# Unread rounded products of 512 columns ahead of the attention scores of a three-layer transformer kernel

## The reference

```python
# first layer
o_gla  = gla_chunked(q, k, v, g)          # 4 heads, dk 64, dv 128, chunks of 64
o_moba = moba_attention(q_b, k_b, v_b)    # 4 heads of 64, causal softmax with ALiBi
o_mem  = memory_attention(q_c, k_c, v)    # 4 heads of 64, 256 memory tokens
x = x + concat(o_gla, o_moba, o_mem) @ w_out
x = x + hierarchical_moe(rmsnorm(x, g), ...)   # 32 experts, 2 of them for each token
# second layer
ya = _diff_attention(...)                 # 4 heads, each with two softmaxes of 64 columns
yb = _dsa_attention(...)                  # 8 heads, 64 keys kept for each query by an index score
x = x + g1 * (concat(ya, yb) @ w_out);  x = x + g2 * swiglu(h)
# third layer
y = _swa_sink_attention(...)              # 16 heads, window of 128
x = x + g1 * (y @ w_out);               x = x + g2 * swiglu(h)
```

## Time and profile before

| what | value |
|---|---|
| time of the kernel, median of 3 runs | 1481.8 us (1477.46 to 1483.74) |
| time of the profiled execution | 1480.7 us |
| span of the profiled execution (first to last instruction) | 1478.7 us |
| PE busy | 1207.3 us, 82% of the span, 7691 MATMUL records |
| DVE busy | 615.7 us, 42% |
| ACT busy | 476.1 us, 32% |
| mean granted PE clock | 0.864 of full speed |
| DMA | 368.67 MB, mean 249 GB/s |

### The profile page before, as it was taken

How to read it: one execution, slowest core, us unless ns; L and a number is a source line. 1 busy time by engine, 2 the same in 40 slices (tenths; PEclk the granted TensorE clock), 3 DMA queues, 4 the chain that set the end, 5 groups by cost and what they waited for, 6 DMA issues and landing times.

```text
span 1478.7 us, 19441 instructions
## 1 busy us (share of the span) xinstructions
PE 1207.3 (82%) x7691; PEld 883.7 (60%) x7691; DVE 615.7 (42%) x1239; ACT 476.1 (32%) x769; POOL 7.6 (1%) x54
## 2 busy tenths in 40 slices
PE   5878886775676756847897888999999978999998
PEld 4655464442333323413675337899898734999986
DVE  3472643110010000101753576655535756565553
ACT  4561530100000000002532335554433447465441
POOL 1000000000000000000000000000000000000000
PEclk9897788888888877977897668899999988999999
DMA  8442347999999999999536431865536462665520
GB/s 292 172 152 76 115 173 320 428 430 429 430 430 428 430 430 428 430 425 403 197 129 228 171 114 58 253 207 201 195 145 226 171 253 90 203 196 174 203 109 29
DMA packets 121728, 368.67 MB, mean 249 GB/s; under 512 B 9842, under 2 KB 56093, under 8 KB 110878
## 3 DMA queue, kind: packets, MB, share of 16 engines
q1 hardware_dynamic: 120556, 367.26, 64.7%
q10 hardware_dynamic: 1074, 0.08, 0.1%
HBM read 366.28 MB, written 1.05 MB: 248 GB/s over the span
## 4 chain that ended last, share of the span: by engine, by line
PE 61%; DMA 21%; DVE 9%; ACT 5%; issue 3%; SPq 1%; DVEq 0%; ACTq 0%
PE ps L1810 58%; DMA more<-in_w_down_dram 7%; DMA more<-in_w_gate_dram 7%; DMA more<-in_w_up_dram 6%; PE ps L1814 3%; DVE st L32 2%; DVE ring_r L32 2%; DVE R_c L32 1%; SPq L664 1%; DVE R_a L32 1%; DVE X_c L32 1%; ACT X_c L32 1%; DVE sc L32 1%; ACT R_a L32 1%; ACT hn L32 1%
## 5 line engine op out<-in xcount | busy, mean ns | idle before, releaser
L1810 PE MATMUL ps<-hT_r,ring_r 128*128 128x256 f32 x864 | 245.5, 284 | 0.0
L1810 PE MATMUL ps<-ring,xg 128*32 128x512 f32 x640 | 140.4, 725 | 121.5 <-DMA more<-in_w_gate_dram 42.6
L1810 PEld LDWEIGHTS ps<-hT_r,ring_r 128*128 128x128 f32 x864 | 167.8, 194 | 0.0
L1810 PEld LDWEIGHTS ps<-ring,xg 128*32 128x32 f32 x640 | 35.2, 131 | 217.2 <-issue 217.2
L32 DVE TENSOR_TENSOR ring_r<-ring,W_c_r 128x1024 fp32r<-128x1024 f32 x94 | 115.2, 1226 | 97.5 <-ACT W_c_r L32 94.1
L1810 PE MATMUL ps<-R_c_r,W_c_r 128*128 128x256 f32 x608 | 153.1, 284 | 0.0
L32 DVE TENSOR_TENSOR ring_r<-ring,X_c_r 128x1024 fp32r<-128x1024 f32 x88 | 107.8, 1225 | 98.4 <-ACT X_c_r L32 95.7
L1810 PE MATMUL ps<-R_c_r,X_c_r 128*128 128x256 f32 x576 | 148.2, 285 | 0.0
L32 ACT ACTIVATE W_c_r<-ring 128x1024 fp32r<-128x1024 f32 x94 | 99.7, 1060 | 89.2 <-PE ps L1810 84.5
L32 ACT ACTIVATE X_c_r<-ring 128x1024 fp32r<-128x1024 f32 x88 | 93.3, 1061 | 90.3 <-PE ps L1810 85.4
L1810 PE MATMUL ps<-hT_r,W_c_r 128*128 128x256 f32 x416 | 119.0, 286 | 1.9 <-DVE R_c_r L32 1.8
(11 more groups left out here) (281 smaller groups left out, 1874.5 us busy)
## 6 DMA issues: line engine op xcount, KB each, us to landing
ring<-in_ada_w_dram SPq DMA_DIRECT2D x24, 2048.0 KB, 8.2
ring<-in_w_gate_dram SPq DMA_DIRECT2D x20, 2048.0 KB, 15.9
ring<-in_w_up_dram SPq DMA_DIRECT2D x20, 2048.0 KB, 20.7
ring<-in_w_down_dram SPq DMA_DIRECT2D x20, 2048.0 KB, 16.4
more<-in_w_up_dram SPq DMA_DIRECT2D x12, 2048.0 KB, 24.4
more<-in_w_gate_dram SPq DMA_DIRECT2D x12, 2048.0 KB, 23.1
more<-in_w_down_dram SPq DMA_DIRECT2D x12, 2048.0 KB, 23.6
ring<-in_ffn_gate_dram SPq DMA_DIRECT2D x22, 1024.0 KB, 5.6
```

Source lines behind the costliest of these rows:

```text
L1810: return pe.matmul(out, lhsT, rhs, start=start, stop=stop, skip_group_check=True)
```

## The change

A helper `keep(b)` is added to PE's program. It multiplies a rounded 128x128 piece of the activations `hT` by a rounded 128x512 piece of them, in one MATMUL, and writes all 512 columns of bank b. It is called ahead of each of the two score products of a unit in the attentions 1, 2 and 3 (48 calls), ahead of each score product of the gated attention (8) and ahead of the values of the gated attention (8): 64 products more. Each bank is overwritten by the product that follows (`start=True`), so that nothing reads what `keep` wrote. The call stands behind `take(b)`; in `gla_values` it stands ahead of the wait for the masked scores. Attention 4 is left as it was.

```diff
+            steady = hH[:, 0:2, :].rearrange("p c n -> p (c n)")
+
+            def keep(b):
+                mm(ps[b][:, :], hH[:, 0, 0:128], steady, True, True)
+
...
                         b = 2 * (U % 2) + m
                         take(b)
+                        if n < 4:
+                            keep(b)
                         mm(ps[b][:, 0:unit.nk], unit.q[m], unit.k[m], True, True).then_inc(s_sc, 1)
...
                 take(u % 4)
                 pe.wait_ge(s_gT, 1)
+                keep(u % 4)
                 mm(ps[u % 4][:, 0:128], gkT[r, hp, 128 * a:128 * a + 128], gqT[r, hp, 128 * a:128 * a + 128], True,
                    True).then_inc(s_gs, 1)
...
                 take(b)
+                keep(b)
                 pe.wait_ge(s_ga, u + 1)
                 pe.wait_ge(s_sst, 6)
```

## The result

The changed kernel takes **1504.5 us** (median of 4 runs, 1503.7 to 1507.0) against 1482.0 (1477.5 to 1483.7): ratio 1.0166, 95% interval 1.0147 to 1.0185, some 24 us slower (the two medians lie 22.5 us apart). I had forecast 1491 with a range that ended at 1504. The direction was right, the size was not. The profiled execution took 1503.7 us with a span of 1501.9, so the two traces are 23.2 us apart.

What follows compares the result with a forecast made beforehand. PE was taken to hold 61% of the chain and DMA 21%, with the experts bound by DMA. Terms -3.2 + 3.6 + 7.5 + 2.7 = +10.6 us on the profiled 1480.7 gave 1491, range 1479 to 1504.

Steps and rivals of the forecast that it cites:

- The price of one product: Each added 512-column product costs 0.23 us at 2.4 GHz and 0.43 at 1.2, read from a stream of rounded products.
- The price of splitting a pair: Parting a unit's two score products costs between 0 and 0.75 us at 256 columns, full clock; 0.45 taken.
- some 3 us: How much higher the whole sum would be if splitting lost the entire second score product, 0.75 instead of 0.45 a unit.
- Gated attention, -3.2: Twelve products on the path cost 2.8 us, attention 1's unit 0 costs 0.8; the held full clock saves 6.8.
- Rival B: Clock falls in the gated attention all the same, so its products do not pay: +21.8 us, 1502; chance 0.28.
- Attention 1, +3.6: Units 1 to 7: 0.9 for unit 1, 0.4 for 2 and 3, 3.6 for 4 to 7, less 1.3 won.
- The run that I had expected to win 1.3: Attention 1's run at 160.43, 3.25 us against 1.92 for another, was to win 1.3 us if the clock holds.
- Attention 2, +7.5: Five of eight units on the chain cost 7.5 us, mostly at half clock; units 0, 4 and 5 hidden by DVE.
- my five units: Attention 2's units 1, 2, 6, 3 and 7, taken as 1.7, 1.4, 1.2, 1.5 and 1.7 us at half clock.
- Attention 3, +2.7: Units 0 to 4 hidden behind DVE from 857 to 876 us; units 5, 6, 7 cost 0.9 us each.
- That a delay of attention 1 shifts the experts by its own length: Experts, 250 to 684 us, are bound by DMA, so delay in gated attention or attention 1 moves the whole block equally.
- Rival C: Clock rises in attentions 2 and 3 as well, so the kernel is not slower: -5.5 us, 1475; chance 0.13.

Runs made afterwards that it cites:

- pair_kept: All 64 products, but in the attentions both of a unit stand ahead of its two scores, unlike the changed kernel; 1.0003 of the kernel before.
- split_only: Kernel before with none of the 64 products, but a one-column float32 product between each unit's two scores in attentions 1 to 3; ratio 1.0198, 29 us slower.
- attention2_and_3: Only the 32 added products of attentions 2 and 3, added to the kernel before; ratio 1.0148, 22 us slower.
- the second trace: The changed kernel run once more, unaltered, for another trace and times: 1515.5 us, ratio 1.0222 to the kernel before at 1480.2.
- gated_twice: Kernel before plus 16 products in the gated attention alone, two adjacent ahead of each values, none ahead of scores; ratio 1.0023.
- paired_early: Kernel before plus two adjacent products ahead of each gated values and, in attention 1, both ahead of each unbroken score pair; ratio 1.0019.

## Why the prediction was right and wrong

*The price of one product, 0.23 us at full clock and 0.43 at half*: wrong. Between two score products it is 0.43 and 0.72. I took it from a stream of rounded products; that row gives what a product costs among its like. The trace before had a closer row that I did not read, the 0.32 us with a score product behind (1183.41), and even that has only one of the two neighbours right.

*The price of splitting a pair, 0.45 us at full clock*: too small. I had bounded it by 0 and 0.75 and chosen between; it is 0.61 to 0.63, the whole second score (`pair_kept` against the change, and `split_only`). The Trainium skill ("TensorE: Matmul & The Clock Gate", Part 3) states that products in different groups of rows run at the same time, the group taking little longer than one, and I had named it as the rule that speaks against the change. The traces agree with it, 0.63 for two and 0.62 for one, and the sum should have gone by it. My "some 3 us" for that rule was itself too low: 0.3 more for each of the 13 units of my sum is 3.9 already, before the half clock. With both prices right a unit of 256 columns costs 1.47 us at full clock, not 0.9, and 2.6 at half (3.74 against 1.16 for the pair), not 1.7; one of 128 columns costs 2.1 at half, not 1.5.

*Gated attention, -3.2*: the mechanism was right, the clock stayed at 1.00 to the end of the stage. The size was off by the price: of the 12 products five cost 0.43 and seven, with a 128-row product behind, 0.34, in all 4.5 us instead of 2.8, and unit 0 cost 1.27 instead of 0.8. And of the 6.8 us, 0.8 lay behind 148.96, in the first run of attention 1, and was won there. That makes -0.2 for the stage; 0.0 was measured. Rival B did not happen, though its number came nearest.

*Attention 1, +3.6*: +4.9 and +8.0 in the two traces. With the true price my sum is +6.5 in place of +3.6; the first run, at full clock now, gives back 0.8 that I had booked to the stage ahead. That leaves 5.7, near the first trace. In the second the clock was lower, 0.84 for 0.90. The run that I had expected to win 1.3 did (161.85 us, 1.92 in the first trace).

*Attention 2, +7.5*: this is the step that failed most, +16.7 and +16.5 in the two traces. Three parts of it were wrong. First the price: my five units make 12.0, not 7.5. Second the cover: units 4 and 5 of attention 2 and unit 0 of attention 3, which I had put behind DVE's work, are on the chain of the changed kernel as well (in its pieces on PE from 835.68, 842.46 and 877.16 us); only unit 0 of attention 2 was hidden. Third the clock, which I had let stand as it was: it fell from 0.62 to 0.55. The same instructions took 68.9 us in `attention2_and_3`, where it was 0.65. So some 10 us are the units at a clock like the one before, and the other 6.5 came only with the lower clock. That more products and a busier PE could leave the clock lower was in none of my cases; `split_only` shows the same, with 0.68 for 0.79 in attention 1. What brings the lower clock about in one execution and not in another stays open. The chain by line, 797 to 904 us before and 803 to 930 after, both from just ahead of the stage to 4 us into the output projection (the view ends its lines there):

```profile
by line: PE ps L1810 40.4%; DVE R_c L32 9.8%; DVE st L32 9.4%; DVE X_c L32 9.3%; issue 7.4%; PE ps L1814 6.8%; ACT X_c L32 3.4%; ACT R_c L32 2.8%; DVE s L32 2.0%; DVE hn L32 1.4%; DVE sc L32 1.3%; DVE ring_r L32 1.2%; DVE modc L32 1.1%; ACT
by line: PE ps L1810 68.3%; PE ps L1814 6.9%; DVE X_c L32 5.0%; issue 4.2%; DVE R_c L32 3.6%; ACT X_c L32 2.1%; DVE st L32 2.0%; ACT R_c L32 1.3%; DVE s L32 1.1%; DVE ring_r L32 1.0%; ACT acc L32 1.0%; ACT W_c_r L32 0.8%; DVE hn L32 0.7%; D
```

*Attention 3, +2.7*: +3.7 and, with the lower clock of the second trace, +7.6. Units 5 to 7 at 1.47 are 4.4. From its first run to the one at 876 nothing was lost in the first trace, as said: 17.6 us before (858.46 to 876.08) and 17.2 after (880.91 to 898.14).

*That a delay of attention 1 shifts the experts by its own length*: right. From the first to the last product of the experts it is 426.2 us before and 426.3 after, and the first comes 4.9 us later (251.87 against 247.02).

*Rival C*, a clock at full in attentions 2 and 3 and no loss, was refuted: attention 2 had 0.55 in both traces, and attention 3 had 0.76 and 0.67, where it had 0.70 before.

## What to carry to other kernels

Before putting anything between two products, look whether they overlap: two products of 64 rows each took the time of one here, and with one product of a single column between them they took 1.57 us instead of 0.63, plus what the clock cost. Take the price of an added instruction from a row in which it has the neighbours that it will have, not from a stream of its like. Filler for the clock belongs ahead of a group that runs together, never inside it. Two adjacent ones are cheaper than two apart, but in the gated attention the clock held in all five traces with them apart and in one of two with them grouped. Whether filler pays has to be seen over many runs and more than one set of them, since all that it won here is a few us at most, in a kernel whose ratio moved by 0.5% from one set of runs to the next.

## What the runs showed that I had not expected

- A busier PE with a lower clock: with pairs split and no filler, attention 1 had PE busy 43.9 of 48.2 us at 0.68, and with pairs together 29.6 of 35.0 at 0.79. A stretch that is busy all the time need not get the full clock, nor one that is less busy lose it.
- The same instructions got a different clock in different executions: the gated attention of `gated_twice` and `paired_early` took 23.8 and 17.0 us, and attention 2 took 69 or 75 with all its products and those of attention 3. What decides it was not found; it stays open.
- Float32 products of 128 columns held the clock like rounded ones of 512 (1.00 in the gated attention in both).
- The price of a product is set by both neighbours: the same rounded product of 512 columns held PE for 0.23, 0.34 or 0.43 us at the full clock.
